# Two weight units fetched between the pieces of the modulation's weights, in a one-layer hybrid encoder step

## The reference

```python
mod = (jax.nn.silu(c) @ w_ada[l] + b_ada[l])[:, None, :]
sh_m, sc_m, g_m, sh_f, sc_f, g_f = jnp.split(mod, 6, axis=-1)
h = rmsnorm(x, norm_mix_w[l]) * (1.0 + sc_m) + sh_m
z, xbc, dt, q, k, v = jnp.split(h @ w_in, SPLITS, axis=-1)
```

## Time and profile before

| | |
|---|---|
| median of 3 runs | 1804.19 us (1802.11 to 1804.35) |
| span of the profiled execution, first to last instruction | 1800.5 us |
| busy share of that span: PE, DVE, ACT, POOL | 91%, 55%, 35%, 25% |
| mean granted clock of PE | 0.956 |
| bytes moved by DMA | 192.25 MB, mean 107 GB/s |

### The profile page before, as it was taken

How to read it: one execution, slowest core, us unless ns; L and a number is a source line. 1 busy time by engine, 2 the same in 40 slices (tenths; PEclk the granted TensorE clock), 3 DMA queues, 4 the chain that set the end, 5 groups by cost and what they waited for, 6 DMA issues and landing times.

```text
span 1800.5 us, 23420 instructions
## 1 busy us (share of the span) xinstructions
PE 1644.2 (91%) x9291; PEld 1451.6 (81%) x9291; DVE 993.5 (55%) x1558; ACT 637.7 (35%) x1150; POOL 441.3 (25%) x261
## 2 busy tenths in 40 slices
PE   5799998699998897787979999999999989998996
PEld 4588896589995665566879999999989978897875
DVE  3775318542015664442567666666556676676744
ACT  4522133111114653352333222223544454444432
POOL 0121124132210000035554332332441121111232
PEclk8899999799997998999989999999999999999998
DMA  9554110231213003626622222222264334443452
GB/s 331 165 177 161 36 26 1 53 84 47 76 49 123 1 1 109 223 67 189 229 96 73 68 59 71 59 65 88 78 176 133 124 99 157 144 144 106 152 164 68
DMA packets 164562, 192.25 MB, mean 107 GB/s; under 512 B 7858, under 2 KB 126875, under 8 KB 164416
## 3 DMA queue, kind: packets, MB, share of 16 engines
q1 hardware_dynamic: 139626, 132.11, 23.9%
q10 hardware_dynamic: 19612, 40.93, 7.1%
q0 software_dynamic: 5216, 17.71, 2.8%
HBM read 173.62 MB, written 17.11 MB: 106 GB/s over the span
## 4 chain that ended last, share of the span: by engine, by line
PE 43%; DVE 5%; DMA 3%; POOL 2%; ACT 1%; issue 1%; ACTq 0%; DVEq 0%
PE PS L624 9%; PE PS L622 9%; PE PS L623 9%; PE PS L1070 4%; PE PS L1071 4%; PE PS L1072 4%; DMA x_rows<-x_scratch 1%; POOL h_lo L2255 1%; PE PS L999 1%; PE PS L1000 1%; DMA x_new<-in_x_prompt_dram 1%; PE PS L1001 1%; DMA weights_raw<-in_w_up_dram 1%; POOL weights_lo L2242 1%; DVE y_new L1563 1%
## 5 line engine op out<-in xcount | busy, mean ns | idle before, releaser
L2242 POOL TENSOR_TENSOR weights_lo<-weights_raw,weights_hi 128x1024 fp32r<-128x1024 f32 x103 | 266.0, 2583 | 814.1 <-ACT weights_hi L1772 814.1
L622 PE MATMUL PS<-h_hi,weights_hi 128*128 128x384 f32 x1280 | 434.9, 340 | 11.6 <-POOL h_lo L2255 7.8
L623 PE MATMUL PS<-h_lo,weights_hi 128*128 128x384 f32 x1280 | 432.1, 338 | 0.0
L624 PE MATMUL PS<-h_hi,weights_lo 128*128 128x384 f32 x1280 | 432.0, 338 | 0.0
L1772 ACT ACTIVATE weights_hi<-weights_raw 128x1024 fp32r<-128x1024 f32 x202 | 213.5, 1058 | 177.6 <-PE PS L1072 106.5
L622 PEld LDWEIGHTS PS<-h_hi,weights_hi 128*128 128x128 f32 x1280 | 242.4, 189 | 20.5 <-issue 19.8
L623 PEld LDWEIGHTS PS<-h_lo,weights_hi 128*128 128x128 f32 x1280 | 242.4, 189 | 0.0
L624 PEld LDWEIGHTS PS<-h_hi,weights_lo 128*128 128x128 f32 x1280 | 242.2, 189 | 0.0
L1070 PE MATMUL PS<-weights_hi,g_hi 128*128 128x512 f32 x396 | 160.8, 406 | 17.8 <-DVE weights_lo L1719 9.0
L2369 POOL TENSOR_TENSOR g_lo<-g_T,g_hi 128x384 fp32r<-128x384 f32 x66 | 81.5, 1236 | 347.9 <-ACT g_hi L2133 347.9
L1071 PE MATMUL PS<-weights_lo,g_hi 128*128 128x512 f32 x396 | 159.2, 402 | 0.0
(11 more groups left out here) (385 smaller groups left out, 2485.6 us busy)
## 6 DMA issues: line engine op xcount, KB each, us to landing
weights_raw<-in_w_up_dram SPq DMA_DIRECT2D x88, 512.0 KB, 4.0
weights_raw<-in_w_down_dram SPq DMA_DIRECT2D x66, 512.0 KB, 4.5
w_ada_unit<-in_w_ada_dram SPq DMA_DIRECT2D x32, 512.0 KB, 5.4
weights_raw<-in_w_in_dram SPq DMA_DIRECT2D x24, 512.0 KB, 5.3
weights_raw<-in_w_out_dram SPq DMA_DIRECT2D x24, 512.0 KB, 3.8
w_ada<-in_w_ada_dram SPq DMA_DIRECT2D x4, 2048.0 KB, 21.5
k_cache<-in_cache_k_dram ACTq DMA_DIRECT2D x8, 1024.0 KB, 5.4
x_rows<-x_scratch ACTq DMA_DIRECT2D x9, 512.0 KB, 4.3
```

The source lines that it names most:

```text
L622: pe.matmul(out, wh, xh, start=(i == 0), stop=False)
L623: pe.matmul(out, wh, xl, start=False, stop=False)
L624: mm = pe.matmul(out, wl, xh, start=False, stop=(i == n - 1))
L2242: mark(gp.tensor_tensor(WL[n % 3][:, :], WR[:, n % 3, :], WH[n % 3][:, :].bitcast(F32), ALU.subtract), "w_lo")
```

## The change

SP's order of transfers in the first stage. The code that fetches a unit becomes a function `unit_in`, and units 0 and 1 are started after the second `w_ada` piece and before the third. Unit 2 stays where it was, behind the fourth piece, and the loop over the rest starts at 2.

```diff
-            for c in range(4):
-                ada_in(c)
+            def unit_in(n):
+                sp.dma_start(WR[:, n % 3, :].rearrange("p (k n) -> p k n", k=KT) if len(units[n].shape) == 3
+                             else WR[:, n % 3, :], units[n]).then_inc(sem(f"w_raw{n % 3}"), 16)
+
+            ada_in(0)
+            ada_in(1)
+            unit_in(0)
+            unit_in(1)
+            ada_in(2)
+            ada_in(3)
...
-            for n in range(NU):
+            for n in range(2, NU):
...
-                sp.dma_start(WR[:, n % 3, :].rearrange("p (k n) -> p k n", k=KT) if len(units[n].shape) == 3
-                             else WR[:, n % 3, :], units[n]).then_inc(sem(f"w_raw{n % 3}"), 16)
+                unit_in(n)
```

## The result

| | before | after |
|---|---|---|
| runs | 22 | 22 |
| median, us | 1799.88 | 1795.60 |
| lowest and highest, us | 1794.45 to 1805.06 | 1787.77 to 1801.50 |
| profiled execution: its time, its span | span 1800.5 | 1790.12, span 1788.3 |

The ratio of the runs after to those before is 0.9972, with a 95% interval of 0.9960 to 0.9985: 5.0 us less, between 2.7 and 7.2. The forecast change was 4.3 us, or 0.24%. The forecast *time*, 1799.9 with a range from 1797.6, was 4.3 us too high and outside its range, because the kernel before is not at 1804.2: those were three of its slower runs. (The medians also differ by 4.3 us. That this equals the forecast is luck, since the interval is 4.5 us wide.)

What follows compares the result with a forecast made beforehand. DVE's chain in the first stage was taken to bound the kernel, by delaying PE's projection. Gains of 2.2 us at ACT and 2.1 at DVE sum to 4.3: 1804.2 - 4.3 = 1799.9 us, range 1797.6 to 1802.6.

Steps and rivals of the forecast that it cites:

- the chain: First stage: DVE's chain sets PE's projection start at 67.33 us, held by ACT's wait for units 0 and 1.
- The 2.2 us on ACT: ACT's h_hi starts at 46.9 instead of 49.11 us, since its roundings no longer wait for units 0 and 1.
- The 2.1 us on DVE: DVE's first L1160 takes 0.62 us instead of 2.70, because POOL's subtractions of units 0 and 1 are done.
- The stretched scale: DVE's scale_cols, both operands in SBUF, waits for POOL until about 46.9 instead of 46.39 us, costing some 0.5.
- the late piece: w_ada piece 3 lands at 48.0 instead of 44.67 us, its PE products end at about 49.9, costing nothing.
- The rival that ended slower: Piece 3 lands at 60.3 us; past 51.2 each microsecond is lost, past 55.5 net loss; time 1809.0, chance 0.04.
- The 3.2 us to spare: Slack between piece 3's products ending on PE at about 49.9 us and their need at 53.1.
- the 0.44: DVE's 0.44 us wait for PE's last sum, which goes if PE's clock stays up through a shorter idle time.
- the 4.7: Total gain in us if PE's clock stays up and DVE's wait for the last sum goes.
- The restart: PE's projection start: 3.2 us at half clock lose 1.6; change taken as zero, plus or minus 1.6 us.
- Rival (3): PE's clock helps as well, 0.44 and up to 1.6 us more: gain 4.7 to 6.3, about 1798.6, chance 0.11.
- the level: Whole kernel: the runs' median before, 1804.2 us, 3.7 above the span of 1800.5, from which 4.3 was subtracted.

Runs made afterwards that it cites:

- One unit alone: Kernel before with only unit 0 fetched between w_ada pieces 1 and 2, unit 1 after piece 3; ratio 0.9990 (0.9971 to 1.0009).
- third trace: The changed kernel run once more, unchanged, with PE's transposes at half clock; ratio to the kernel before 0.9973, median 1793.21 us.
- first trace: The profiled execution of the changed kernel in the result; time 1790.12 us, span 1788.3 us.
- six spare products: Changed kernel plus six unused 128x256 products on PE behind the fifth tile's transposes; PE's projection started at 59.73 us in its trace.

## Why the prediction was right or wrong

**Right: the chain.** DVE's modulation bounded the stage, ACT's wait for the pair of units held it, and PE had no gap behind it. One unit alone gave 1.0 us, and nothing that the projection gained was given back before 240 us.

**Right: both terms.** The 2.2 us on ACT: `h_hi` at 46.86 in the execution with the same clock in the transposes, 46.9 forecast. The 2.1 us on DVE: 2.70 to 0.62, and shown to be POOL's by taking POOL's work away. The stretched scale, 0.5 forecast, took 0.36 more than its 0.20, and ended 0.06 behind POOL (in the third trace it came 0.24 before POOL's end and took 0.29). The Trainium skill's rule ("GPSIMD Engine Reference", section 8, Key points) of two SBUF inputs is borne out: the PSUM copies kept 0.69, and the two-SBUF-input scale did not keep its 0.20.

**Right: the late piece.** It landed at 48.04 for 48.0, and with 7 us more it gave everything back. The rival that ended slower had its point about right, and its price too low by the 1.3 us of clock. The 3.2 us to spare were there in the execution with the clock that the sum had; in the first trace it was 1.8 us, and with six spare products nothing. The earlier the stage runs, the nearer this rival comes.

**Small term: the 0.44.** PE's idle time ahead of the sums fell to 1.8 to 3.2 us, and the sums took 1.95 to 2.31 us instead of 3.58, so DVE did not wait. That is the 4.7, which I had as an upper case and which came in all three traces of the changed kernel. The restart cost 0.38 x 4.74 = 1.8 us in the first trace and 0.50 x 4.89 = 2.4 us in the third, against 1.6: near a draw, as assumed. The Trainium skill ("TensorE: Matmul & The Clock Gate", Part 1) has the throttled state as the default and the point of transition as different from run to run. The traces agree: PE's clock was 1.00 up to 53.0 us after the short wait, and the restart was at half clock from the start in the first trace of before and from 68.8 us on in the second.

**Missed: what the bound becomes.** The sum took one execution's PE times as fixed. I wrote that ACT would wait for the scale, and did not follow the scale back to PE's transposes, whose clock differs by execution. Taking the transfer away did not just subtract 4.3; it tied the stage to an earlier event that is up to 1.4 us sooner in some runs. The mechanism was right, its size low by 0.4 to 1.8 us in the three traces of the changed kernel. Rival (3), 4.7 to 6.3 us, had the size, but for the clock of the sums and of the restart and not of the transposes.

**Wrong: the level.** The step that failed is the last line of the sum, "the runs' median stood 3.7 above the span, so 1804.2 - 4.3". Three runs, 2.2 us apart, were taken as the kernel's level, and their spread as its spread. 22 runs of it have a median of 1799.88 and a spread of 10.6 us. From there the same 4.3 us gives 1795.6, which is what was measured, to a tenth by luck. Also, every run on record stands about 1.8 us above its own span (1790.12 and 1788.3), so the 3.7 was no constant: the profiled execution itself took about 1802.3 by that, and the rest of the 3.7 compared it with the median of others. The range allowed for the clock at one restart, 1.6 us, where the trace of before, in windows of 1 us, has 24 stretches at half clock.

## What to carry to other kernels

Find the first instruction that waits for a transfer ahead of work that others wait for, and ask what is in the queue before it that has slack; here 1 MB moved past 4 MB, and the whole cost, 3.4 us on a piece with over 6 us to spare in the trace of before, was free. When such a wait goes, sum up again from the event that is now last, in its fast and its slow form, instead of subtracting. And give a change and a level apart: a change of 0.3% can be read from one stage's rows, while the level of three runs was off by as much as the change was worth.

## What the runs showed of the hardware

- One kernel's runs differ by 0.9% (1792.35 to 1808.80), in step with the mean granted clock of TensorE (0.962 to 0.952).
- Requests of one queue landed one behind the other, 1.7 us for a 0.5 MB unit and 5.6 us for a 2 MB piece; an exchange in the order shifted the landing of piece 3 by 3.4 us, to 48.04, and left unit 2's at 49.8.
- A DVE instruction with two SBUF operands that falls into a POOL tensor_tensor waits for its end (0.20 became 2.32, and 0.62 became 2.13 and 2.70), and can get in between two of them; one that reads PSUM did not wait (0.69 with POOL and without).
- With four unused 128x256 products, 1.99 us in an idle gap of 4 us, the next stage ran at full clock from its start in one trace (1.00 in its first window, where three traces without them have 0.50, 0.62 and 0.69 in theirs).
